# Who makes the remainders of the gated values: VectorE or GpSimd, in the expert combination of a two-layer encoder

## The reference, cut to what matters

```python
def expert_block(args):
    xb, eb, gb = args
    ub = jnp.take(u, eb, axis=0)
    a = jax.nn.gelu(jnp.einsum('td,tkd->tk', xb, ub), approximate=False) * gb
    vb = jnp.take(v, eb, axis=0)
    return jnp.einsum('tk,tkd->td', a, vb)
```

## Time and profile before

| what | us |
|---|---|
| median of 3 runs | 1566.06 (1563.86 to 1566.98) |
| the profiled execution | 1563.96 |
| its span, first to last instruction | 1562.1 |
| TensorE, VectorE busy in the span | 1533.4, 1382.6 |
| ScalarE, GpSimd busy in the span | 657.0, 628.6 |

### The profile page before, as it was taken

How to read it: one execution, slowest core, us unless ns; L and a number is a source line. 1 busy time by engine, 2 the same in 40 slices (tenths; PEclk the granted TensorE clock), 3 DMA queues, 4 the chain that set the end, 5 groups by cost and what they waited for, 6 DMA issues and landing times. The chain is left out here.

```text
span 1562.1 us, 28238 instructions
## 1 busy us (share of the span) xinstructions
PE 1533.4 (98%) x10798; PEld 1481.4 (95%) x10798; DVE 1382.6 (89%) x2612; ACT 657.0 (42%) x1197; POOL 628.6 (40%) x437
## 2 busy tenths in 40 slices
PE   9999999999999999999999999999999999999997
PEld 8988999999999999999988889999999999999996
DVE  6987997989998999998966779898999989999996
ACT  5563222333324444545635441233333354444452
POOL 5651005744442656555003200256444435555520
PEclk9999999999999999999999999999999999999999
DMA  7644569999999999999843246799999999999991
GB/s 251 235 136 135 191 220 353 375 402 389 374 367 390 371 392 407 409 409 408 305 170 108 69 147 243 254 389 370 403 380 371 379 367 406 409 407 409 409 378 60
DMA packets 136966, 493.96 MB, mean 316 GB/s; under 512 B 16064, under 2 KB 16576, under 8 KB 136576
## 3 DMA queue, kind: packets, MB, share of 16 engines
q1 hardware_dynamic: 85248, 307.42, 52.8%
q0 software_dynamic: 47552, 170.06, 28.3%
q10 hardware_dynamic: 4032, 14.68, 2.7%
HBM read 488.79 MB, written 1.05 MB: 314 GB/s over the span
## 5 line engine op out<-in xcount | busy, mean ns | idle before, releaser
L700 POOL DMA_INDIRECT big<-v,picks x160 | 279.7, 1748 | 240.3 <-DVE big L1965 186.6
L700 POOL DMA_INDIRECT big<-u_rows,picks x160 | 223.9, 1400 | 238.5 <-DVE big L1880 211.7
L634 DVE TENSOR_TENSOR low<-raw,high 128x1024 fp32r<-128x1024 f32 x194 | 242.2, 1252 | 30.5 <-ACT high L1270 30.3
L738 PE MATMUL work<-columns,raw 128*128 128x176 f32 x1600 | 249.1, 313 | 3.4 <-DVE big L1858 3.4
L738 PEld LDWEIGHTS work<-columns,raw 128*128 128x128 f32 x1600 | 240.1, 190 | 4.2 <-issue 4.1
L1270 ACT ACTIVATE high<-raw 128x1024 fp32r<-128x1024 f32 x209 | 218.4, 1048 | 45.6 <-PE work L738 11.6
L1965 DVE SCALAR_TENSOR_TENSOR big<-big,side_hid 128x1024 f32<-128x1024 f32 x156 | 199.6, 1280 | 1.3
L1880 DVE SCALAR_TENSOR_TENSOR big<-big 128x1024 f32<-128x1024 f32 x160 | 190.5, 1220 | 11.0 <-DMA big<-u_rows,picks 11.0
L758 PE MATMUL work<-xT,high 128*128 128x352 f32 x704 | 196.8, 357 | 0.9 <-DVE big L1858 0.9
L874 PE MATMUL y<-xT,high 128*128 128x352 f32 x656 | 195.0, 359 | 1.3 <-DVE xT L1935 0.6
L874 PE MATMUL work<-xT,high 128*128 128x352 f32 x656 | 191.3, 354 | 0.0
(11 more groups left out here) (267 smaller groups left out, 2982.3 us busy)
## 6 DMA issues: line engine op xcount, KB each, us to landing
raw<-v SPq DMA_DIRECT2D x156, 512.0 KB, 8.1
raw<-u SPq DMA_DIRECT2D x150, 512.0 KB, 7.1
extra_raw<-u SPq DMA_DIRECT2D x106, 512.0 KB, 6.8
extra_raw<-v SPq DMA_DIRECT2D x100, 512.0 KB, 9.3
raw<-wq SPq DMA_DIRECT2D x32, 512.0 KB, 3.8
raw<-conv_in SPq DMA_DIRECT2D x14, 512.0 KB, 4.6
aux<-ln_par ACTq DMA_DIRECT2D x9, 512.0 KB, 9.3
raw<-conv_out SPq DMA_DIRECT2D x8, 512.0 KB, 3.8
```

The costliest lines, as they stand in the source:

```text
L634: ops.tensor_tensor(low_at(c), raw_at(c), high_at(c).bitcast(F32), ALU.subtract).then_inc(low_made[RAW_SLOT[c]], 1)
L700: nc.gpsimd.indirect_dma_start(out=side_rows[n % SIDE_BUFS], out_offset=None, in_=rows, in_offset=bass.IndirectOffsetOnAxis(ap=pick_ids[:, ...
L738: mm = nc.tensor.matmul(out_, raw_at(c)[:, k * P:(k + 1) * P], x_full[:, k, :], start=(k == 0), stop=(k == KD - 1))
```

## The change

No v block is full any more: `FULL_V` is empty, so all 128 of a layer are split. And the remainders of the gated values of blocks 3 to 122 (`POOL_A`, 120 in a layer) are made by GpSimd instead of VectorE, with a semaphore of their own. Blocks 0 to 2 and 123 to 127 stay with VectorE. GpSimd issues the first 85 gathers of a layer as before. The other 75 are issued in a loop over the v blocks: in each, first the gather whose buffer the side sum of that block sets free, then the remainder of the block three ahead. TensorE waits on whichever semaphore goes with the block; the attention's weight loads wait for both.

```diff
-FULL_V = [_n for _n in range(FIRST_COLUMNS, COLUMNS - LAST_COLUMNS) if _n % 6 == 3]
+FULL_V = []
+POOL_A = [_n for _n in range(RING, COLUMNS - LAST_COLUMNS - 1 + RING) if _n not in FULL_V]
...
+A_RANK_POOL = [sum(_m in POOL_A for _m in range(_n + 1)) for _n in range(NKEYS)]
+A_RANK_DVE = [_a - _b for _a, _b in zip(A_RANK, A_RANK_POOL)]
...
-                for n in range(2 * SIDE_ROWS):
+                for n in range(SIDE_ROWS + SIDE_BUFS):
                     gather(n)
...
+                for block_n in range(COLUMNS):
+                    summed = SIDE_SUMS_AT.get(block_n)
+                    if summed is not None and summed + SIDE_BUFS < SIDE_ROWS:
+                        gather(SIDE_ROWS + SIDE_BUFS + summed)
+                    n = block_n + RING
+                    if n in POOL_A:
+                        pool.wait_ge(a_high, A_BLOCKS * layer + A_RANK[n])
+                        nc.gpsimd.tensor_tensor(xT_low[:, n % KD, 0:DT], hid[:, n, :],
+                                                xT_high[:, n % KD, 0:DT].bitcast(F32),
+                                                ALU.subtract).then_inc(a_low_pool, 1)
...
+                def wait_a(n):
+
+                    if n in POOL_A:
+                        pe.wait_ge(a_low_pool, A_RANK_POOL[-1] * layer + A_RANK_POOL[n])
+                    else:
+                        pe.wait_ge(a_low, A_RANK_DVE[-1] * layer + A_RANK_DVE[n])
...
                     if c not in FULL:
-                        pe.wait_ge(a_low, A_BLOCKS * layer + A_RANK[c - first])
+                        wait_a(c - first)
...
-                    act.wait_ge(a_low, A_BLOCKS)
+                    act.wait_ge(a_low, A_RANK_DVE[-1])
+                    act.wait_ge(a_low_pool, A_RANK_POOL[-1])
...
                     for next_block in a_after(c):
-                        a_lo(layer, next_block - v0)
+                        if next_block - v0 not in POOL_A:
+                            a_lo(layer, next_block - v0)
```

More of the change, by code:

```diff
@@ L445, in program @@
         a_high = sem("a_high_made")
-        a_low = sem("a_low_made")
+        a_low = sem("a_low_made_by_vector")
+        a_low_pool = sem("a_low_made_by_gpsimd")
         x_ready = [sem("x_half_0_normalised"),
```

## The result

The changed kernel takes 1640.8 us (median; 1639.1 to 1642.8) against 1566.5 before: ratio 1.0475, 95% interval 1.0450 to 1.0499, so 74 us slower. The profiled execution took 1639.64 us, its span 1637.8.

The account below looks back on a forecast made before the run. VectorE, stopped by GpSimd's remainders, was to replace TensorE as the v stage's bound: 2 x (23.4 + 7 for GpSimd's order) + 7.1 for angle steps - 0.9 = +67 us, predicted 1632 us, range 1590 to 1695.

Parts of the forecast that it names:

- GpSimd's tensor_tensor stops VectorE: In the v stage, GpSimd's remainders, which read SBUF, hold up VectorE's two-input instructions for a whole instruction; 0.38 to 0.55 us each.
- The hold, 0.40 us a remainder: Time VectorE is stopped by each GpSimd remainder; 109 x 0.40 = 43.6 us in blocks 4 to 112 of a layer.
- The extra low halves: Splitting 40 full v blocks gives VectorE 40 more L634 at 1.14 us; 20.5 us in blocks 4 to 112 of each layer.
- VectorE becomes the bound: In blocks 4 to 112, VectorE needs 263.9 us where these blocks now take 240.5; +23.4 us a layer.
- VectorE near 100%: Sign of rightness: VectorE near 100% busy in the v stages, with its waits for GpSimd counted.
- The order on GpSimd, 7 us a layer: GpSimd's remainders and gathers queue behind each other in the v stage; missed turns cost 7 us a layer, up to 31.
- The angle steps, +7 us in layer 0: VectorE's eight L2009 and eleven small steps in layer 0 no longer find slack; +7.1 us.
- DMA below 380 GB/s, landing back to 6 or 7 us: Sign of rightness in the v stage: DMA rate falls below 380 GB/s and loads land in 6 or 7 us.
- Rival B: GpSimd's short remainder does not stop VectorE, TensorE stays the bound in the v stage; -8.8 us, about 1556; chance 0.11.

Follow-up runs that it names:

- the kernels without the order term: Changed kernel without the 75 later gathers of each layer, 1604.6 us; changed kernel with the remainder before the gather in each block, 1610.2 us.

## Why the prediction was right, and where it was not

The time was: 1632 foretold, 1640.8 measured; +67 us in the sum, +74 measured. Of its steps:

- *GpSimd's tensor_tensor stops VectorE.* Right: with a memset instead, 68 of 74 us are gone and L638 is at 1.22 us; with half the columns VectorE's records grow by less than half as much. The Trainium skill (SBUF — State Buffer, section "SBUF: two separate sides") names an exclusive lock, held for the whole instruction, between a VectorE instruction with two SBUF inputs and a GpSimd instruction that reads SBUF. The trace agrees with this: 0.36 us more on an L638 beside a subtraction, nothing beside a memset.
- *The hold, 0.40 us a remainder.* A little too large: 0.31 us in layer 0, where the angle steps are held up for 3.8 us besides, and 0.35 in layer 1. In the sum this is about 38.5 us a layer instead of 43.6, so 10 us too much over both layers.
- *The extra low halves.* Right in size: the sum gives +21 us for splitting alone, measured +24.7. By layer it is less exact: 14 and 7 us foretold, 12.9 and 14.2 measured, with the one wait of 6 us in layer 1 that no term had.
- *VectorE becomes the bound.* Right only for the kernels without the order term, where it is busy 216 to 218 of 220 us and the time is 1605 to 1610, +39 and +45. In the changed kernel it is at 208 of 220, as before, and TensorE waits for `xT`, not for `low`. The sign set down for rightness, VectorE near 100%, did not appear.
- *The order on GpSimd, 7 us a layer.* This is the step that failed. The walk through one block gave GpSimd 2.74 us and VectorE 2.74, took the race as mostly won and let the three blocks of lead absorb the misses. Turning the order gains 29 us, so the term is 15 us a layer, twice the value taken and half of the upper end. A remainder that is ready stood behind a gather that waited for a side sum and then for a turn.
- *The angle steps, +7 us in layer 0.* It holds where VectorE is the bound: with the order turned layer 0 loses 8.3 us more than layer 1, without the gathers 8.2. In the changed kernel it is only 2.5. No run isolates them.
- *DMA below 380 GB/s, landing back to 6 or 7 us.* Right: 350 GB/s, and 6.2 us for loads issued between 640 and 660:

```profile
DMA to landing us min/median/max: 4.8/6.2/6.8
```

- *Rival B's gain of 8.8 us* would not have come in full: 3 us with everything else out of the way.

So the number is in part luck. The hold was 10 us too large and the order 15 too small; with both put right the sum gives +72, and the forecast came close because the two errors are of opposite sign. Its mechanism was half of the truth: the holds are there, but in the changed kernel GpSimd's queue, and not VectorE's sum, makes TensorE wait.

Four of the runs form a square (us over before):

| | memset | subtraction |
|---|---|---|
| gather first | +6 | +74 |
| remainder first | -3 | +45 |

With a memset the order costs 9 us, with the subtraction 29. So the order is dear mainly because gather and remainder both wait for VectorE. The ladder by parts: splitting alone 25; with remainders on GpSimd in the good order 45; in the order of the change 74. The middle step fits the holds: 0.35 us of VectorE a remainder, the angle steps' part included, instead of the 0.25 of its own make 22 us over 2 x 110 blocks.

The point that the forecast missed, though it stood in its numbers: the offload could not win even on VectorE alone. The engine gave away an instruction of 0.25 us and was stopped for 0.31 to 0.35.

## What to carry to other kernels

Before moving a small elementwise operation from VectorE to GpSimd, compare what it costs VectorE with what GpSimd's version would stop VectorE for: here both read SBUF, and the second is the larger. When an engine's queue holds urgent and less urgent work that wait for the same neighbour, put the urgent one first; that alone was worth 29 us here, and 37 with the full blocks. And when two engines are at 95 to 100%, see what the next limit is (here probably the DMA engines, at 408 GB/s) before pricing a gain on the first.

## What was not expected of the hardware

Between gathers and VectorE the hold-up goes one way. In the run without full blocks, with VectorE busy 218 of 220 us, an indirect gather takes 2.34 us on average, where one took 0.94 at 530.16 us of the kernel before. VectorE's L1986 and L638 stay at 1.28 and 1.22 us beside them:

```profile
L704 POOL DMA_INDIRECT big<-v,picks x68 | 158.8, 2336 | 62.5 <-DVE big L1986 62.2 <-issue 0.3
```
